# A streaming hybrid encoder layer on one core: the table that says how much of the expert stage's work stands beside each step of the other stages

## The reference, cut to what matters

```
    g = jax.nn.softmax(top, axis=-1)
    act = jax.nn.gelu(jnp.einsum('nhkd,nd->nhk', peer_u[eid], h).astype(jnp.float32))
    w = (g * act).astype(h.dtype)
    return jnp.einsum('nhk,nhkd->nd', w, peer_v[eid])
```

## Time and profile before

| | us |
|---|---|
| median of 3 runs | 5373.57 |
| lowest, highest | 5368.92, 5374.9 |
| the profiled execution's own time | 5381.02 |
| its span, first to last instruction | 5379.2 |

### The profile page before, as it was taken

How to read it: one execution, slowest core, us unless ns; L and a number is a source line. 1 busy time by engine, 2 the same in 40 slices (tenths; PEclk the granted TensorE clock), 3 DMA queues, 4 the chain that set the end, 5 groups by cost and what they waited for, 6 DMA issues and landing times.

```text
span 5379.2 us, 46425 instructions
## 1 busy us (share of the span) xinstructions
PE 3461.5 (64%) x16090; PEld 1728.5 (32%) x16090; DVE 2777.6 (52%) x6532; ACT 931.4 (17%) x2005; POOL 2546.9 (47%) x2347
## 2 busy tenths in 40 slices
PE   5787989803988867774188888878681233343355
PEld 3355655502544533332044434544240000000000
DVE  2233321698755542469945555543569745445430
ACT  2243210101542210001034442210010000000000
POOL 0000000033476654454476576645453677777775
PEclk8798999956998988886599999988885555555555
DMA  5765234345998988786699898987785799999998
GB/s 223 267 248 186 92 116 125 122 156 200 312 386 313 353 300 292 280 333 240 233 370 366 304 362 326 344 296 286 278 326 183 282 412 389 413 420 400 419 400 308
DMA packets 443015, 1568.01 MB, mean 291 GB/s; under 512 B 48328, under 2 KB 87624, under 8 KB 433184
## 3 DMA queue, kind: packets, MB, share of 16 engines
q0 software_dynamic: 336352, 1224.89, 60.2%
q1 hardware_dynamic: 104528, 338.51, 17.3%
q10 hardware_dynamic: 1904, 1.65, 0.1%
HBM read 1521.72 MB, written 43.14 MB: 291 GB/s over the span
## 4 chain that ended last, share of the span: by engine, by line
PE 43%; DVE 20%; DMA 17%; POOL 9%; issue 7%; ACT 4%; ACTq 0%; SPq 0%; DVEq 0%; POOLq 0%
DMA peer_v_ring<-in_peer_v,expertsT 14%; PE bank L2263 6%; PE wide L1720 6%; POOL peer_v_ring L2205 5%; POOL peer_u_ring L2197 4%; DVE peer_u_ring L2345 4%; PE bank L1720 4%; PE bank L709 3%; PE wide L1973 3%; PE wide L1333 3%; PE wide L1322 2%; PE wide L774 2%; PE wide L784 2%; PE wide L1836 1%; PE bank L719 1%
## 5 line engine op out<-in xcount | busy, mean ns | idle before, releaser
L2197 POOL DMA_INDIRECT peer_u_ring<-in_peer_u,experts x1152 | 1312.8, 1140 | 1335.0 <-DVE peer_u_ring L2345 923.5
L2345 DVE SCALAR_TENSOR_TENSOR peer_u_ring<-peer_u_ring,peer_h 128x1024 f32<-128x1024 f32 x1152 | 1366.1, 1223 | 543.5 <-DMA peer_u_ring<-in_peer_u,experts 490.5
L2263 PE MATMUL bank<-peer_v_ring,peer_lone 128*32 128x512 f32 x4608 | 868.9, 851 | 1073.8 <-DMA peer_v_ring<-in_peer_v,expertsT 1046.4
L2205 POOL DMA_INDIRECT peer_v_ring<-in_peer_v,expertsT x1152 | 1211.5, 1052 | 486.1 <-issue 282.2
L2263 PEld LDWEIGHTS bank<-peer_v_ring,peer_lone 128*32 128x32 f32 x4608 | 125.4, 127 | 1702.0 <-issue 1662.7
L2166 POOL MEMSET peer_lone<- 128x1087 f32 x1 | 1.0, 1003 | 981.7 <-SPq L267 981.7
L709 PE MATMUL bank<-hT,w_ring 128*128 128x384 f32 x768 | 266.8, 498 | 17.1 <-DMA w_ring<-in_weights 15.8
L1333 PE MATMUL wide<-w_ring,hT 128*128 128x256 f32 x1152 | 258.2, 385 | 14.8 <-DVE gla_v L1645 14.8
L1107 DVE SCALAR_TENSOR_TENSOR sb_l<-sb_z,sb_l 128x768 f32<-128x768 f32 (+2 forms) x120 | 96.1, 801 | 330.0 <-ACT sb_l L989 330.0
L1973 PE MATMUL wide<-mT,w_ring 128*128 128x384 f32 x768 | 263.8, 499 | 3.0 <-DMA w_ring<-in_weights 3.0
L1333 PEld LDWEIGHTS wide<-w_ring,hT 128*128 128x128 f32 x1152 | 220.9, 193 | 62.8 <-issue 33.0
(11 more groups left out here) (276 smaller groups left out, 4647.6 us busy)
## 6 DMA issues: line engine op xcount, KB each, us to landing
w_ring<-in_weights SPq DMA_DIRECT2D x312, 512.0 KB, 6.3
sb_kc<-in_kcT SPq DMA_DIRECT2D x16, 2048.0 KB, 11.7
sb_vc<-in_vc SPq DMA_DIRECT2D x16, 2048.0 KB, 7.3
mod_w<-in_w_ada SPq DMA_DIRECT2D x24, 1024.0 KB, 6.6
peer_u_ring<-in_peer_u,experts POOLq DMA_INDIRECT x1152, 6.4
peer_v_ring<-in_peer_v,expertsT POOLq DMA_INDIRECT x1152, 6.4
norm_x<-in_x SPq DMA_DIRECT2D x9, 512.0 KB, 5.4
oB<-sb_oT SPq DMA_DIRECT2D x24, 192.0 KB, 5.5
```

The costliest lines, as they stand in the source:

```text
L2197: pool.indirect_dma_start(self.u_ring[:, n % NU, :], None, K.A["peer_u"], bass.IndirectOffsetOnAxis(ap=K.ids_of[:, j % 6, k:k + 1], axis=0 ...
L2205: pool.indirect_dma_start(self.v_ring[:, m % NV, :], None, K.A["peer_v"], bass.IndirectOffsetOnAxis(ap=K.ids_of_turned[:, j % 6, t:t + 1], ...
L2263: last = pe.matmul(self.F.psum[strip:strip + 32, :], self.lone[:, mark - at:mark - at + 32], self.v_ring[:, m % NV, c * HALF:(c + 1) * HAL ...
L2345: dve.scalar_tensor_tensor(u, u, 1.0, self.h2[:, j % 2, :], ALU.mult, ALU.mult, accum_out=self.dots[:, j % 2, k:k + 1]).then_inc(self.dot_ ...
```

## The change

The line that spreads a stretch evenly is replaced. Before, the slots of a stretch were spread over its ticks in proportion to their weights. Now a tick of w estimated us is given w / 1.7 slots until the slot number that ends the stretch is reached, and none after that.

```diff
-MARGIN, SLOT_US, AHEAD, CONSTS = 14, 2.6, 6, 12
+MARGIN, SLOT_US, FIRST_US, AHEAD, CONSTS = 14, 2.6, 1.7, 6, 12
@@ def paces():
-        total, done = sum(units[here:stop]), 0.0
+        done = 0.0
         for w in units[here:stop]:
             done += w
-            out.append(int(before + span * min(1.0, done / total)))
+            out.append(int(before + min(span, done / FIRST_US)))
```

## The result

The changed kernel takes 5614.64 us (median of 4 runs, 5608.62 to 5627.83) against 5374.23 of the kernel before: a ratio of 1.0451, with a 95% interval of 1.0428 to 1.0473. I had forecast 5426, and 5510 at most. The direction was right, the size was not: +240 us where the sum gave +53. The execution that was profiled took 5627.83 us, 247 more than the one of before.

What follows compares the result with a forecast made beforehand. DMA was taken to bound the tail and the fuller stick stages, DVE late select, with mix waiting for v gathers. Stage terms summed to +53 us, giving 5426 us from the median of runs; range 5324 to 5510.

Steps and rivals of the forecast that it cites:

- (a): Select, last two tiles: more slots at 1.19 us of DVE each, +25 in group 0 and +28 in group 1.
- (d): Mix, res and first select of group 1: 116 slots go away, 551 us becomes 351, -200.
- (g): Mix, res and first select of group 2: 523 us becomes 351, -172.
- the hold: Mix to first select runs without slots and gets its time back at once: -200 and -172 us.
- group 0's 351 us: Time of mix, res and first select without any slot, taken as what groups 1 and 2 would fall to.
- How fast DMA gives when all of it is asked for is the unknown: DMA's rate in stick and gla, bracketed by 371 and 404 to 420 GB/s, taken as 394.
- (b): Stick of group 1: 194 slots instead of 130, 99 plus 387 us against 343, +143.
- (c): Gla of group 1: 99 slots, 315 us plus 21 us free, 336 against 285, +51.
- (e): Stick of group 2: 245 slots instead of 154, 273 MB at 394 GB/s, 692 us against 543, +149.
- DMA gives less, or the chain of a step adds to it: Rival, chance 0.10: at 371 GB/s in group 2 and 375 in gla, about +125, 5500 us.
- side estimate by the 358 GB/s: The sum over all stages with HBM's limit from the skill page as DMA's rate: about +220 us.
- DMA gives more: Rival, chance 0.26: DMA reaches 420 GB/s in stick and gla, sum about -50, 5324 us.

Runs made afterwards that it cites:

- e18: Changed kernel with gathers of half rows (512 of 1,024 numbers), on a chip like the first: 5695.78 us against 5373.85 for the kernel before.
- e17: Changed kernel with dots that only sum the gathered row (one SBUF input), on a chip like the first: 5493.14 us against 5373.85 for the kernel before.
- e12: Changed kernel with gathers of 64 rows instead of 128, on a slower chip: 5768.95 us against 5516.31 for the kernel before, ratio 1.0455.
- e7: Changed kernel with half-row gathers, sum-only dots, rings of fourteen and issue thirteen slots ahead: 5710.38 us against 5497.28 for the kernel before.
- e5: Changed kernel without any expert gather, dots and pairs kept on zeros: 4534.70 us against 5497.28 for the kernel before.
- e6: Kernel before without any expert gather, dots and pairs kept on zeros: 4440.57 us against 5497.28 with gathers.
- e9: The changed kernel itself, run again as a control on a slower chip: 5744.44 us against 5516.31 for the kernel before, ratio 1.0411.

## Why the prediction went wrong, by its steps

**Right.** Term (a), the dots' price in select: +25 and +29 against +25 and +28. Terms (d) and (g), the hold: -196 and -170 against -200 and -172, so group 0's 351 us was the right measure for mix without slots (352 and 351 in the finer cut). The tail's length. The direction, and that no engine but the supply of gathers bounds the burst: PE is busy for 572 of 786 us, its clock at 0.88 (0.82 in group 1).

**The step that failed** is "How fast DMA gives when all of it is asked for is the unknown", and with it terms (b), (c) and (e): the burst was priced by bytes at 394 GB/s, "since each engine behind it has time left but DMA has none". GpSimd stood in front of DMA and was never priced. The earlier trace rows had its busy time: 722 us in the tail with 733 instructions is 0.98 each, and the tail's lines above add 0.30 behind each. The tail's 404 GB/s, which I read as DMA's limit, are 524,288 bytes each 1.29 us (406). In e18, half the bytes in the same number of gathers didn't shorten the tail.

By the right price: term (e) is 498 gathers at 1.18 + 0.30 us, 737, and 49 of waits for PE and DVE: 786, where 692 was taken. Term (b), 426 us in place of 387 after slot 138: 323 busy, 78 in gaps and 26 in waits. Term (c), 367 in place of 336: 242 busy, 60 in gaps and 50 in waits for buffers, so in gla the issue alone doesn't account for the miss. Stick and gla of group 1 came out 41 and 31 us too low, norm, stick and gla of group 2 12, 94 and 12, together 190, and 53 + 190 = 243 against 247 measured.

**The rivals.** "DMA gives less, or the chain of a step adds to it" came nearest of them, with +125, by a wrong mechanism: its 371 GB/s came true in stick (364 to 377), as a result of what GpSimd asked for. The prediction's side estimate by the 358 GB/s of the Trainium skill, +220, is closer still to the measured 240. That is luck: e17 moved 391 GB/s in the same stage and 414 in the tail. "DMA gives more" was out of reach in this kernel: at 1.24 us a gather GpSimd can ask for 423 GB/s at most, and at the 1.48 of stick for 354, to which the dense stages add some 22 (17.5 MB in 786 us). The Trainium skill has two statements that point at the step, neither with a price. "GPSIMD Engine Reference" of the Trainium skill, section Specifications, says that GpSimd's SBUF interfaces are shared with VectorE, with contention when a VectorE instruction has two inputs in SBUF, as each dot has. The trace agrees: 0.94 against 1.83 and 1.99 us. With dots of one input (e17) the mean is 0.97, and of the 34 gathers in stick of group 2 that still take over 1.1 us, 32 stand beside L1107, a dense operation with two inputs in SBUF. "DMA: Bandwidth & Descriptors" of the Trainium skill, section SWDGE vs HWDGE vs iDMA, says that software on GpSimd computes the descriptors of such transfers. A cost by instruction and not by byte fits that; that half the rows save no more than 0.19 us of an instruction is e12's measurement.

**What stays open.** Which part of the 200 us that gathers add to stick of group 2 is GpSimd's and which is DMA's. In e17 GpSimd is taken for 625 of 754 us by gathers and gaps and waits for buffers for 126, while DMA's share is 0.99; half the bytes and dots of one input together were not run on a chip like the first. Nor were half the rows or longer rings. Why increments come late on three of the chips is not known either; that they follow trains of gathers is read from traces, and no experiment was made on it. Why gathers with half the bytes stretch more in the tail (1.24 us for v against 0.99) isn't known: dots overlap them no more there, 0.47 us of each on average in e18 against 0.45 in the kernel before. So a dot beside a gather doesn't always make it long, and what decides it was not found.

## What to carry to other kernels

Price a stream of gathers by the instruction on the engine that issues it, gap and stretch included, before pricing its bytes. If GB/s times the time of one instruction and its gap gives its size, the issuer may be the bound and not DMA; half the bytes in as many instructions tells which. Add the "issue" gaps to a busy share before calling it slack. And where a stage waits because work comes in lumps larger than its ring, cut the lump; moving the work to a stage whose supply is already full costs more than the wait did.

## What the runs showed of the hardware

- A gather of 128 rows takes GpSimd 0.94 us and a gap of 0.30, as long for rows of 2,048 as of 4,096 bytes. Issued beside dots with two inputs in SBUF it takes up to 1.99 us, 1.18 on average in stick of group 2; beside sums with one, 0.94 to 0.98 on average.
- DMA gave 414 GB/s over 910 us in the tail of e17, to one core, with hardly anything but gathers.
- The kernel before takes 5374 to 5381 us in three of six sets of runs and 5492 to 5516 in three others, on other chips. On the slower ones, some instructions start up to 10.6 us after the recorded end of what they wait for, around trains of gathers (e7); kernels without gathers show no such wait there (e5, e6). The changed kernel's tail takes 1232 us on such a chip (e9) and 1126 on the first.
